# A two-layer encoder trunk: one more fast pair per feed-forward stage, and another order at the stages' edges

## The chip, the cores and the metric

The kernel runs on one core of a Trainium2 chip. The metric is the device time of one execution in microseconds; the figure shown for a kernel is the median of its runs. The profile is of one further execution.

## The reference: what is computed

Two layers work on `x` of 512 tokens by 1024 features, in float32. Each layer is a token mixer (gated linear attention in layer 0, chunked attention in layer 1) and then a feed-forward part, each followed by a LayerNorm of `alpha * x + y`. The change touches the feed-forward part, which both layers have:

```python
def swiglu(x, w_in, w_out):
    gate, up = jnp.split(x @ w_in, 2, axis=-1)
    return (jax.nn.silu(gate) * up) @ w_out
```

`w_in` is 1024 by 5632 (2816 gate columns, 2816 up columns), `w_out` is 2816 by 1024.

## The kernel before

Each float32 operand of a matmul is split into a high part, which ScalarE (ACT) makes by a copy with rounding, and a low part, the difference, made by VectorE (DVE) or GpSimd (POOL). A product is then three matmuls on TensorE (PE): high by high, high by low, low by high (`three`, L1603 to L1605).

**The weight stream.** All weights come in slabs of 128 by 1024, two to a transfer, issued by SyncE into a ring of two places, `raw`. SyncE issues the next transfer when both slabs of the one two before it have their high and low parts (`hi_done`, `lo_done`). The high and low parts lie in rings of four slabs, `w_hi` and `w_lo`. `split_hi` (L497, ACT) and `split_lo` (L967, POOL) are the usual makers. The first four slabs of some stages have places of their own ("early" slabs) and are split ahead of the stage.

**The first half of a feed-forward stage** has 22 pairs of column blocks, one gate and one up block of 128 columns each; a pair is one transfer. The first `PLAIN` = 4 pairs are done the classical way: 2 blocks by 8 depth tiles by 3 matmuls of 512 tokens, 48 matmuls. Pairs 0 and 1 are the early slabs, done in two token halves; pairs 2 and 3 go through the ring. The other `FAST` = 18 pairs are done by a Strassen scheme (Winograd's form): seven products of half the depth and half the tokens, 7 by 4 by 3 = 84 matmuls of 256 tokens. I call them plain and fast pairs.

**What a fast pair needs.** From `x`: four sums of its blocks, formed once a stage on DVE in `sum_x` (L1162 to L1178); the fourth, `t4_sum`, takes L1177 and L1178. ACT makes the high parts of the first three (L579), DVE the low parts (L1301); the fourth gets its high part at L677 (ACT) and its low part at L1313 (DVE), after the last plain pair, because it replaces a block of x that plain pairs still read. From the weights: DVE forms sums (L1201, L1203, L1209, L1212), ACT the high parts (L585 for the gate slab, L589, L593, L597, L601), DVE the low parts (L1218, L1224, L1230, L1235), POOL one low part, `form_a22_low` (L986). These lie in two sets of places, `w_s32` and `w_s4`, by the parity j of the pair.

**The order of products in a fast pair** (PE, `pair`): 1 to bank a, 2 to bank f, 3 to bank a again, 4 to bank e, 5 to bank a, 6 to bank g, 7 to bank a. Bank a is used four times, so ACT copies it out in between: `copy_p1` (L609) after product 1, awaited by product 3; `copy_u2` (L613) after 3, awaited by 5; `copy_u4` (L621) after 5, awaited by 7. The result of 7 is read by `gate_late` (L633). DVE adds the other banks: `gate_of_early` (L1242) feeds ACT's `gate_early` (L625). The engines run ahead by one pair: in `pair(i, j)` ACT and DVE also form the weights of the next pair, in an order that is written out by hand, the same for all pairs but the last.

**The second half** is `out_projection` on 22 slabs of `w_out`. ACT's `hidden_high` (L565) and DVE's `hidden_low` (L1185) split the hidden activations; the high parts lie in a ring of six. The last fast pair of a stage has no next pair: there ACT splits the first slabs of `w_out` and the first hidden blocks. The last four slabs of the second half (`TAIL`) are gone through token tile by token tile. In layer 0 the four early slabs of the next stage are split in its iteration `k = 14`, ahead of those last four.

Of the kernel before, what the change touches and what calls it, by code (L numbers as in the profile page):

```python
# [29 lines left out]
P = 128  # L30
# [52 lines left out]
PLAIN = 4  # L83
# [24 lines left out]
def build_program(nc, a):  # L108
    ctx = ExitStack()
    with ctx:  # L110
# [89 lines left out]
        def halves_at(name, shape, hi, lo):  # L200
# [6 lines left out]
        w_s32 = [halves_at("w_s32_0", [P, 2, HALF], region + 76 * KB, region + 44 * KB),  # L207
                 halves_at("w_s32_1", [P, 2, HALF], region + 68 * KB, gb_at)]
        w_s4 = [halves_at("w_s4_0", [P, HALF], region + 80 * KB, region + 82 * KB),
                halves_at("w_s4_1", [P, HALF], region + 72 * KB, region + 74 * KB)]  # L210
# [198 lines left out]
        def blocks_of(n0, j):  # L409

            slot = (n0 + 2 * j) % RING
            return slot, slot + 1, (n0 // 2 + j) % RAWS
# [59 lines left out]
        def _(act):  # L472
# [55 lines left out]
            def out_projection(n0, slabs, ln):  # L528

                banks = LN_BANKS[ln]  # L530
                for k in range(slabs - TAIL):
                    if slabs == KF and k + HI_RING < KF:
                        hidden_high(ln // 2, k + HI_RING)
# [3 lines left out]
                    split_hi(n0 + k + RING)  # L537

# [28 lines left out]
            def feed_forward(f, n0):  # L567
# [35 lines left out]
                def copy_p1(i, j, start):  # L603
                    act.wait_ge(multiplied[f], i * 12 + (6 * j + 1))
                    if start:
                        act.wait_ge(prod_done[f], PLAIN - 1 + j)
                    else:
                        act.wait_ge(half_prod[f], i * 4 + (2 * j - 3))
# [26 lines left out]
                def pair(i, j, start, before_start, last=False):  # L635
# [11 lines left out]
                    else:  # L647
                        form_s32_high(i_next, j_next)
                        form_s1_high(i_next, j_next)
                        form_a22_high(i_next, j_next)  # L650
                    copy_u2(i, j)
                    if last:
                        split_hi(FFN_OUT[f] + 1)
                        hidden_high(f, 2)
                        hidden_high(f, 3)
                    else:
                        form_s4_high(i_next, j_next)
# [8 lines left out]
                split_hi(n0 + RING + 2)  # L666
                split_hi(n0 + RING + 3)
                gate(2)
# [5 lines left out]
                gate(3)  # L674
# [7 lines left out]
                with act.Fori(2, FAST // 2 - 1) as i:  # L682
                    pair(i, 0, False, False)
                    pair(i, 1, False, False)
                pair(FAST // 2 - 1, 0, False, False)
                pair(FAST // 2 - 1, 1, False, False, True)
                hidden_high(f, 4)
                hidden_high(f, 5)
                gate_late(FAST // 2 - 1, 1, False)
# [260 lines left out]
        def _(pool):  # L950
# [30 lines left out]
            def feed_forward(f, n0):  # L981
# [11 lines left out]
                with pool.Fori(1, FAST // 2) as i:  # L993
                    form_a22_low(i, 0)
                    form_a22_low(i, 1)
                for n in range(n0 + 2 * KF, n0 + 2 * KF + RING):
                    split_lo(n)
# [1155 lines left out]
```

## Time and profile before

| what | us |
|---|---|
| median of 3 runs | 1184.44 (1184.26 to 1184.64) |
| the profiled execution's own time | 1181.81 |
| its span, first to last instruction | 1180.1 |
| PE busy | 1156.9 |
| DVE, ACT, POOL busy | 647.6, 528.2, 419.5 |

The profiled execution's own time is 1.7 us over its span and 2.6 us under the median. The mean granted TensorE clock is 0.997 of full speed. Differences of stretches are read from the trace and taken from the own time; the same difference is then taken from the median.

### The profile page before, as it was taken

The page shows a single profiled execution, that of the slowest core. Times are in us where ns is not written, and L with a number is a line of the kernel's source. Part 1 is how long each engine was busy: PE and PEld are TensorE (multiplying, and loading weights), DVE is VectorE, ACT ScalarE, POOL GpSimd, SP SyncE. Part 2 cuts the span into 40 slices and gives each one's busy share as a digit, 9 for nine tenths or more (in the row PEclk, how much of TensorE's full clock was granted, in tenths as well). Part 3 has the DMA queues.
Part 4 walks back from the last instruction along what each step waited for, and adds up shares of the span by engine and source line. Part 5 has one row for each costly group of instructions (what it writes and reads, how often), then busy time and mean ns, then how long its engine had stood idle before and what let it go on. Part 6 is the DMA issues. An engine that isn't in the chain of part 4 may idle for free.

```text
span 1180.1 us, 18906 instructions
## 1 busy us (share of the span) xinstructions
PE 1156.9 (98%) x6958; PEld 1020.3 (86%) x6958; DVE 647.6 (55%) x1173; ACT 528.2 (45%) x918; POOL 419.5 (36%) x247
## 2 busy tenths in 40 slices
PE   8999999999999999999999999999999999999997
PEld 6887888989999997887887777778989999988886
DVE  4070173788888863112604676636888888841105
ACT  4354253345555553223425666662455555542222
POOL 2438426141111124446245334471311111144441
PEclk9999999999999999999999999999999999999999
DMA  6433314232222233324032212131222333232221
GB/s 217 171 132 107 107 36 143 79 136 101 97 96 101 104 107 143 107 78 172 19 107 72 90 50 85 57 143 60 72 73 107 107 107 107 107 141 80 101 72 72
DMA packets 21977, 119.89 MB, mean 102 GB/s; under 512 B 2449, under 2 KB 6673, under 8 KB 8993
## 3 DMA queue, kind: packets, MB, share of 16 engines
q1 hardware_dynamic: 15440, 104.96, 25.3%
q10 hardware_dynamic: 6480, 14.17, 3.6%
q8 instruction: 37, 0.61, 0.2%
q14 instruction: 20, 0.16, 0.0%
HBM read 117.02 MB, written 5.24 MB: 104 GB/s over the span
## 4 chain that ended last, share of the span: by engine, by line
PE 89%; DVE 4%; ACT 3%; POOL 2%; DMA 1%; issue 1%; SPq 0%; DVEq 0%; POOLq 0%; ACTq 0%
PE bank L1603 27%; PE bank L1605 27%; PE bank L1604 27%; PE bank L1994 2%; PE bank L1979 2%; POOL s_w_lo L967 1%; PE bank L1665 1%; DMA s_raw<-stream 1%; DVE s_g_c L1382 1%; PE bank L2015 1%; PE bank L2014 1%; PE bank L1863 1%; DVE s_a_lo L1185 1%; ACT s_w_hi L497 1%; PE bank L1856 0%
## 5 line engine op out<-in xcount | busy, mean ns | idle before, releaser
L967 POOL TENSOR_TENSOR s_w_lo<-s_raw,s_w_hi 128x1024 fp32r<-128x1024 f32 x108 | 266.1, 2474 | 314.3 <-ACT s_w_hi L497 314.3
L1603 PE MATMUL bank<-s_t_hi,s_w_hi 128*128 128x256 f32 (+1 forms) x832 | 265.7, 319 | 2.8 <-ACT s_gate_s L613 2.2
L1605 PE MATMUL bank<-s_t_hi,s_w_lo 128*128 128x256 f32 (+1 forms) x832 | 263.2, 316 | 0.0
L1604 PE MATMUL bank<-s_t_lo,s_w_hi 128*128 128x256 f32 (+1 forms) x832 | 262.9, 316 | 0.0
L986 POOL TENSOR_TENSOR s_w_lo<-s_raw,s_w_hi 128x512 fp32r<-128x512 f32 x36 | 64.8, 1800 | 307.0 <-ACT s_w_hi L597 307.0
L1603 PEld LDWEIGHTS bank<-s_t_hi,s_w_hi 128*128 128x128 f32 x832 | 158.8, 191 | 12.7 <-DVE s_w_lo L1218 2.5
L1605 PEld LDWEIGHTS bank<-s_t_hi,s_w_lo 128*128 128x128 f32 x832 | 158.7, 191 | 10.5
L1604 PEld LDWEIGHTS bank<-s_t_lo,s_w_hi 128*128 128x128 f32 x832 | 158.9, 191 | 9.3
L497 ACT ACTIVATE s_w_hi<-s_raw 128x1024 fp32r<-128x1024 f32 x111 | 115.6, 1054 | 114.5 <-PE bank L1605 87.1
L1603 PE MATMUL bank<-s_w_hi,s_a_hi 128*128 128x512 f32 x352 | 138.0, 392 | 1.5 <-POOL s_w_lo L967 1.3
L1604 PE MATMUL bank<-s_w_lo,s_a_hi 128*128 128x512 f32 x352 | 137.4, 390 | 0.0
L1605 PE MATMUL bank<-s_w_hi,s_a_lo 128*128 128x512 f32 x352 | 137.3, 390 | 0.0
L1185 DVE TENSOR_TENSOR s_a_lo<-s_act_a,s_a_hi 128x512 fp32r<-128x512 f32 x44 | 36.1, 832 | 168.6 <-ACT s_a_hi L565 168.6
L1603 PE MATMUL bank<-s_t_hi,s_w_s_hi 128*128 128x256 f32 x432 | 122.8, 284 | 4.4 <-ACT s_prod L621 4.4
L1605 PE MATMUL bank<-s_t_hi,s_w_s_lo 128*128 128x256 f32 x432 | 122.7, 284 | 0.0
L1604 PE MATMUL bank<-s_t_lo,s_w_s_hi 128*128 128x256 f32 x432 | 122.7, 284 | 0.0
L1603 PE MATMUL bank<-s_w_hi,s_t_hi 128*128 128x512 f32 x288 | 113.9, 396 | 2.7 <-DVE s_t_lo L1339 1.3
L1605 PE MATMUL bank<-s_w_hi,s_t_lo 128*128 128x512 f32 x288 | 112.3, 390 | 0.0
L1604 PE MATMUL bank<-s_w_lo,s_t_hi 128*128 128x512 f32 x288 | 112.2, 389 | 0.0
L1603 PEld LDWEIGHTS bank<-s_t_hi,s_w_s_hi 128*128 128x128 f32 x432 | 83.3, 193 | 4.8 <-ACT s_prod L621 4.8
L1605 PEld LDWEIGHTS bank<-s_t_hi,s_w_s_lo 128*128 128x128 f32 x432 | 83.3, 193 | 0.0
L1604 PEld LDWEIGHTS bank<-s_t_lo,s_w_s_hi 128*128 128x128 f32 x432 | 83.3, 193 | 0.0
(200 smaller groups left out, 2053.6 us busy)
## 6 DMA issues: line engine op xcount, KB each, us to landing
s_raw<-stream SPq DMA_DIRECT2D x97, 1024.0 KB, 4.7
s_ln_gb<-ln_gb ACTq DMA_DIRECT2D x4, 1024.0 KB, 4.5
bias_rows<-rel_bias ACTq DMA_DIRECT2D x1, 3072.0 KB, 12.4
s_h<-x ACTq DMA_DIRECT2D x1, 2048.0 KB, 12.7
s_r_b<-bias_rows ACTq DMA_DIRECT2D x16, 128.0 KB, 2.3
s_x_t<-x_t ACTq DMA_DIRECT2D x3, 512.0 KB, 11.9
out<-s_h SPq DMA_DIRECT2D x3, 512.0 KB, 2.6
s_raw<-stream SPq DMA_DIRECT2D x2, 256.0 KB, 5.4
```

The lines of the kernel that those rows point to most:

```text
L497: nc.scalar.activation(w_parts(n, slice(0, SLAB))[0], raw[:, pair % RAWS, n % 2, :], ACT.Copy).then_inc(hi_done, 2 if n == 1 else 1)
L967: nc.gpsimd.tensor_tensor(lo, raw[:, place // 2 % RAWS, n % 2, :], hi.bitcast(F32), ALU.subtract).then_inc(lo_done, 2 if n == 1 else 1)
L986: nc.gpsimd.tensor_tensor(w_lo[:, up_at, HALF:], raw[:, slot, 1, HALF:], w_hi[:, up_at, HALF:].bitcast(F32), ALU.subtract).then_inc(lo_don ...
L1185: nc.vector.tensor_tensor(a_lo[:, k, :], act_a[:, k, :], a_hi[k % HI_RING][:, :].bitcast(F32), ALU.subtract).then_inc(a_lo_done[f], 1)
L1382: nc.vector.tensor_tensor_scan(g_c[:, hd, :], keep[:, :], g_c[:, hd, :], 0.0, ALU.mult, ALU.add).then_inc(cum_done, 1)
L1603: nc.tensor.matmul(out, l_hi, r_hi, start=start, stop=False, skip_group_check=skip)
L1604: nc.tensor.matmul(out, l_hi, r_lo, start=False, stop=False, skip_group_check=skip)
L1605: return nc.tensor.matmul(out, l_lo, r_hi, start=False, stop=stop, skip_group_check=skip)
L1665: last = nc.tensor.transpose(bank[banks[t][half]][:, k * P:(k + 1) * P], src[:, t, (4 * half + k) * P:(4 * half + k + 1) * P], ident[:, :])
L1863: last = nc.tensor.matmul(bank[GLA_O_BANKS[t][hd // 2]][:, (hd % 2) * GLA_DV:(hd % 2 + 1) * GLA_DV], g_am[:, t % 2, hd * P:(hd + 1) * P], ...
L1979: last = nc.tensor.matmul(bank[2 + hd][:, keys], qk[q][rows, toks], qk[k][rows, keys], start=(i == 0), stop=(i == 2))
L1994: last = nc.tensor.transpose(bank[4 + hd][:, at * P:(at + 1) * P], r_p[:, s % 4, j * P:(j + 1) * P], ident[:, :])
```

## The change

`PLAIN` goes from 4 to 3, so that each feed-forward stage has 3 plain and 19 fast pairs; the odd last fast pair is written out, and the two sets of places `w_s32` and `w_s4` change roles. The second half of the fourth sum of x becomes `add_x4`, which DVE does after the weights of the first fast pair. In the first fast pair ACT does `copy_u2` ahead of the next pair's high parts. In the last fast pair ACT does `copy_u4` ahead of `gate_early` and of two of the hidden blocks' high parts, and DVE does two `hidden_low` ahead of `gate_of_early` where it did four. In the second half ACT does `split_hi` ahead of `hidden_high` in each iteration; for `k = 14` of layer 0 this puts the four early slabs and the slab itself ahead of `hidden_high`.

```diff
-PLAIN = 4
+PLAIN = 3
...
         def blocks_of(n0, j):
-            slot = (n0 + 2 * j) % RING
-            return slot, slot + 1, (n0 // 2 + j) % RAWS
+            slot = (n0 + 2 * (PLAIN + j)) % RING
+            return slot, slot + 1, (n0 // 2 + PLAIN + j) % RAWS
...
                 for k in range(slabs - TAIL):
-                    if slabs == KF and k + HI_RING < KF:
-                        hidden_high(ln // 2, k + HI_RING)
                     if ln == 1 and k == slabs - 2 * TAIL:
                         for j in range(TAIL):
                             split_hi(n0 + slabs + j)
                     split_hi(n0 + k + RING)
+                    if slabs == KF and k + HI_RING < KF:
+                        hidden_high(ln // 2, k + HI_RING)
...
                 def copy_p1(i, j, start):
                     if start:
-                        act.wait_ge(prod_done[f], PLAIN - 1 + j)
+                        act.wait_ge(prod_done[f], PLAIN)
...
                 def pair(i, j, start, before_start, last=False):
...
                         hidden_high(f, 0)
                         hidden_high(f, 1)
                         split_hi(FFN_OUT[f])
-                    else:
-                        form_s32_high(i_next, j_next)
-                        form_s1_high(i_next, j_next)
-                        form_a22_high(i_next, j_next)
-                    copy_u2(i, j)
-                    if last:
+                        copy_u2(i, j)
                         split_hi(FFN_OUT[f] + 1)
-                        hidden_high(f, 2)
-                        hidden_high(f, 3)
-                    else:
-                        form_s4_high(i_next, j_next)
+                        copy_u4(i, j, start)
+                        gate_early(i, j)
+                        return
+                    if before_start is None:
+                        copy_u2(i, j)
+                    form_s32_high(i_next, j_next)
+                    form_s1_high(i_next, j_next)
+                    form_a22_high(i_next, j_next)
+                    if before_start is not None:
+                        copy_u2(i, j)
+                    form_s4_high(i_next, j_next)
                     gate_early(i, j)
                     copy_u4(i, j, start)
...
                 gate(1)
-                split_hi(n0 + RING + 2)
-                split_hi(n0 + RING + 3)
-                gate(2)
                 form_plain_high(0, 0)
                 form_s32_high(0, 0)
                 form_s1_high(0, 0)
                 form_a22_high(0, 0)
                 form_s4_high(0, 0)
-                gate(3)
+                gate(2)
...
-                pair(FAST // 2 - 1, 0, False, False)
-                pair(FAST // 2 - 1, 1, False, False, True)
-                hidden_high(f, 4)
-                hidden_high(f, 5)
-                gate_late(FAST // 2 - 1, 1, False)
+                pair(FAST // 2, 0, False, False, True)
+                hidden_high(f, 2)
+                gate_late(FAST // 2, 0, False)
+                for k in range(3, HI_RING):
+                    hidden_high(f, k)
                 split_hi(FFN_OUT[f] + 2)
                 split_hi(FFN_OUT[f] + 3)
...
                 own(nc.vector.tensor_tensor(t4_sum[:, :, :], t_hi[:, KD // 2:, EARLY_TOKS].bitcast(F32), t2[:, :, :], ALU.subtract))
+
+            def add_x4(f):
+
                 nc.vector.tensor_tensor(t4_sum[:, :, :], t4_sum[:, :, :], t_lo[:, KD // 2:, EARLY_TOKS].bitcast(F32),
                                         ALU.add).then_inc(x_summed[f], 1)
-                dve.wait_ge(x_summed[f], 4)
...
                     if last:
-                        for k in range(HI_RING - 2):
+                        for k in range(2):
                             hidden_low(f, k)
...
                 plain_prod(1)
-                plain_prod(2)
                 sums_31(0, 0)
                 sums_24(0, 0)
                 form_plain_low(0, 0)
                 form_s32_low(0, 0)
                 form_s1_low(0, 0)
                 form_s4_low(0, 0)
-                plain_prod(3)
+                add_x4(f)
+                plain_prod(2)
                 dve.wait_ge(x_sum_hi[f], 4)
...
-                for c in range(RING):
+                for c in range(2 * PLAIN - RING):
                     pe.wait_ge(lo_done, n0 + RING + c + 1)
```

## Rows read from the trace of the kernel before

**Rows 1.** The page's first part: busy time of each engine, its share, instructions

```profile
PE 1156.9 (98%) x6958; PEld 1020.3 (86%) x6958; DVE 647.6 (55%) x1173; ACT 528.2 (45%) x918; POOL 419.5 (36%) x247
```

**Rows 2.** Waits of PE in the whole run: us in total, times, longest

```profile
PE bank L1603 <- ACT s_prod L621: 4.4, 2, 2.2
PE bank L1603 <- ACT s_gate_s L613: 2.2, 2, 1.1
...
PE bank L1603 <- POOL s_w_lo L967: 2.0, 3, 0.7
```

**Rows 3.** Windows: us, PE, PEld, DVE, ACT, POOL busy (instructions), clock, DMA share, GB/s

```profile
252.35:263.23 10.88, 10.88 (x49) 9.01 (x48) 7.86 (x9) 4.29 (x6) 1.88 (x1) 1.00 0.24 85
263.23:274.61 11.38, 10.30 (x86) 10.12 (x85) 10.26 (x15) 5.96 (x10) 1.89 (x1) 1.00 0.17 50
274.61:284.69 10.08, 10.08 (x87) 10.08 (x86) 8.33 (x14) 5.41 (x10) 1.78 (x1) 1.00 0.36 127
435.89:448.41 12.52, 10.33 (x87) 10.13 (x86) 7.32 (x11) 6.85 (x13) 5.25 (x2) 1.00 0.22 75
546.35:554.14 7.79, 6.32 (x25) 4.28 (x24) 0.00 (x0) 1.99 (x2) 6.26 (x3) 1.00 0.46 144
...
1038.43:1051.63 13.20, 11.01 (x86) 10.80 (x85) 8.01 (x12) 6.85 (x13) 5.25 (x2) 0.94 0.26 95
...
1050.13:1053.40 3.27, 3.27 (x14) 2.88 (x13) 2.07 (x5) 1.80 (x4) 0.13 (x1) 0.50 0.68 286
```

**Rows 4.** Timeline of DVE, start of the fast pairs in layer 0: start, us, line

```profile
240.97 3.31 DVE L1178 TENSOR_TENSOR s_t_sum<-s_t_sum,s_t_lo 128x1024 f32<-128x1024 f32 x1
...
244.92 4.97 DVE L1301 TENSOR_TENSOR s_t_lo<-s_t_sum,s_t_hi 128x1024 fp32r<-128x1024 f32 x3
...
253.16 0.69 DVE L1201 TENSOR_TENSOR s_w_s_sum<-s_raw 128x512 f32<-128x512 f32 x1
...
258.09 1.79 DVE L1230 TENSOR_TENSOR s_w_lo<-s_s_sum,s_w_hi 128x512 fp32r<-128x512 f32 x1
259.80 0.68 DVE L1235 TENSOR_TENSOR s_w_s_lo<-s_w_s_sum,s_w_s_hi 128x512 fp32r<-128x512 f32 x1
...
264.53 1.23 DVE L1313 TENSOR_TENSOR s_t_lo<-s_t_sum,s_t_hi 128x1024 fp32r<-128x1024 f32 x1 [0.40 <-ACT s_t_hi L677]
...
270.60 0.41 DVE L1242 TENSOR_TENSOR s_gate_s<-s_gate_s,bank 128x256 f32<-128x256 f32 x1
```

**Rows 5.** Timeline of ACT, the same stretch

```profile
255.21 1.06 ACT L589 ACTIVATE s_w_s_hi<-s_w_s_sum 128x1024 fp32r<-128x1024 f32 x1 [1.24 <-DVE s_w_s_sum L1209]
...
263.43 1.06 ACT L677 ACTIVATE s_t_hi<-s_t_sum 128x1024 fp32r<-128x1024 f32 x1 [4.84 <-PE bank L1605]
...
265.35 0.36 ACT L609 ACTIVATE s_gate_s<-bank 128x256 f32<-128x256 f32 x1
...
269.72 0.36 ACT L613 ACTIVATE s_gate_s<-bank 128x256 f32<-128x256 f32 x1
```

**Rows 6.** Timeline of POOL, the same stretch

```profile
240.39 6.15 POOL L967 TENSOR_TENSOR s_w_lo<-s_raw,s_w_hi 128x1024 fp32r<-128x1024 f32 x2 [0.54 <-ACT s_w_hi L497]
257.44 1.88 POOL L986 TENSOR_TENSOR s_w_lo<-s_raw,s_w_hi 128x512 fp32r<-128x512 f32 x1 [10.90 <-ACT s_w_hi L597]
```

**Rows 7.** Timelines of DVE and ACT, last fast pair of layer 0

```profile
442.29 3.48 DVE L1185 TENSOR_TENSOR s_a_lo<-s_act_a,s_a_hi 128x512 fp32r<-128x512 f32 x2 [2.53 <-ACT s_a_hi L565]
...
446.46 0.36 ACT L621 ACTIVATE s_prod<-bank 128x256 f32<-128x256 f32 x1
```

**Rows 8.** Timelines of ACT and POOL, end of layer 0's second half

```profile
530.77 1.99 ACT L497 ACTIVATE s_early<-s_raw 128x1024 fp32r<-128x1024 f32 x2
...
541.60 1.06 ACT L497 ACTIVATE s_w_hi<-s_raw 128x1024 fp32r<-128x1024 f32 x1 [5.83 <-DMA s_raw<-stream]
...
542.74 9.87 POOL L967 TENSOR_TENSOR s_w_lo<-s_raw,s_w_hi 128x1024 fp32r<-128x1024 f32 x4 [1.37 <-ACT s_w_hi L497]
```

**Rows 9.** The page's DMA issues: count, KB each, us to landing

```profile
s_raw<-stream SPq DMA_DIRECT2D x97, 1024.0 KB, 4.7
```

More of the change, by code:

```diff
@@ L206, in build_program @@
                   for name, hi, lo in (("t1", 48, 52), ("t2", 56, 60), ("t3", 64, 84))}
[L207 to L210, printed above, removed]
+        w_s32 = [halves_at("w_s32_0", [P, 2, HALF], region + 68 * KB, gb_at),
+                 halves_at("w_s32_1", [P, 2, HALF], region + 76 * KB, region + 44 * KB)]
+        w_s4 = [halves_at("w_s4_0", [P, HALF], region + 72 * KB, region + 74 * KB),
+                halves_at("w_s4_1", [P, HALF], region + 80 * KB, region + 82 * KB)]
         t4_sum = sb_at("t4_sum", [P, KD // 2, SEQ // 2], F32, prod_at)
@@ L681, in feed_forward @@
                 pair(1, 1, False, False)
-                with act.Fori(2, FAST // 2 - 1) as i:
+                with act.Fori(2, FAST // 2) as i:
                     pair(i, 0, False, False)
                     pair(i, 1, False, False)
-                pair(FAST // 2 - 1, 0, False, False)
-                pair(FAST // 2 - 1, 1, False, False, True)
-                hidden_high(f, 4)
-                hidden_high(f, 5)
-                gate_late(FAST // 2 - 1, 1, False)
+                pair(FAST // 2, 0, False, False, True)
[3 more added lines that the diff above has]
+                    hidden_high(f, k)
                 split_hi(FFN_OUT[f] + 2)
@@ L995, in feed_forward @@
                     form_a22_low(i, 1)
+                form_a22_low(FAST // 2, 0)
                 for n in range(n0 + 2 * KF, n0 + 2 * KF + RING):
@@ L1316, in feed_forward @@
                 pair(0, 1, True)
-                with dve.Fori(1, FAST // 2 - 1) as i:
+                with dve.Fori(1, FAST // 2) as i:
                     pair(i, 0, True)
                     pair(i, 1, True)
-                pair(FAST // 2 - 1, 0, True)
-                pair(FAST // 2 - 1, 1, True, True)
-                up_of_late(FAST // 2 - 1, 1)
-                up_of_early(FAST // 2 - 1, 1)
-                hidden_early(FAST // 2 - 1, 1)
-                for k in range(HI_RING - 2, HI_RING):
-                    hidden_low(f, k)
-                hidden_late(FAST // 2 - 1, 1)
-                for k in range(HI_RING, KF):
+                pair(FAST // 2, 0, True, True)
+                up_of_late(FAST // 2, 0)
+                up_of_early(FAST // 2, 0)
+                hidden_early(FAST // 2, 0)
+                hidden_low(f, 2)
+                hidden_late(FAST // 2, 0)
+                for k in range(3, KF):
                     hidden_low(f, k)
@@ L1798, in feed_forward @@
                     pair(i, 1, False)
+                pair(FAST // 2, 0, False)
             pe.wait_ge(am_zeroed, 1)
```

## The prediction

> **What bounds the kernel now.** I read the page's busy times first: PE is busy 98% of the span, the next engine 55% [rows 1]. So time is had only by giving PE less work, or by filling its idle stretches. Second come the waits of PE, for the whole run: three kinds belong to places that the change touches, the longest two of them twice each, once per layer [rows 2]. PE waits for `copy_u4` (L621), 2.2 us a time, for `copy_u2` (L613), 1.1 us a time, and for `split_lo` (L967), some of it at the end of layer 0's second half. Third, the windows put a price on each place, as start-to-start time of PE's work, which also holds what an idle stretch costs beside the idle itself [rows 3]. A fast pair in the middle takes 10.08 us; the first one of layer 0 takes 11.38, the last one 12.52, the last one of layer 1 13.20. Last, the timelines of DVE, ACT and POOL at these places say who was late and behind what [rows 4 to 8].
>
> **1. One plain pair becomes a fast pair.** Plain: 10.88 us for 48 matmuls of 512 tokens. Fast: 10.08 us for 84 of 256 [rows 3]. That is -0.80 us a layer, -1.6 in all. The fast pair brings 14 DVE instructions (8.33 us) and 10 of ACT (5.41), both under 10.08, so the steady state hides them; the transfers are the same slabs. Swapping the two sets of places costs nothing: it puts the last pair (now j = 0) again on the set that the hidden blocks' ring does not overlap. The Trainium skill's page "TensorE: Matmul & The Clock Gate", section "Back-to-back issue gap", gives N/2.4 + 2.5 ns a matmul when nothing else binds, 109 ns at 256 and 216 at 512. By it the exchange would be worth 1.19 us a layer instead of 0.80, and the total 0.8 us lower; the rows have 120 and 227 ns, and I go by them.
>
> **2. The start of the fast pairs.** Today the first fast pair loses 11.38 - 10.08 = 1.30 us: DVE forms the second pair's sums only after L1313, so ACT's L589 is late, and `copy_u2` stands behind it at 269.72, where product 5 was ready to start at 268.99 (four products of 1.44 us after 263.23) [rows 3, 5]. The change puts `copy_u2` in front, and this loss goes: -1.3 a layer.
>
> But the first fast pair now starts 10.88 us earlier, at 252.35, and its preparation must be there. I lay DVE out again from 240.97, where L1178 started [rows 4]. `plain_prod(0)` takes it to 241.6. The three L1301 took 4.97 us because POOL held them up until 246.54 (240.39 + 6.15) [rows 4, 6]; those two POOL instructions are the splits of plain pair 3 and are gone. Alone such an instruction takes 1.23 (L1313) [rows 4] and the next starts after 1.14, so three end at 245.0. The Trainium skill, "SBUF — State Buffer", section "SBUF: two separate sides", calls the port pair of VectorE and GpSimd an exclusive lock for two-input instructions. If the lock were not what stretched the three, they would still take 4.97 and everything below would be 1.55 us later in each layer; the rows (blocked to POOL's end, then 1.1 each) fit the lock.
>
> `plain_prod(1)` ends at 245.6. The chain that began at 253.16 follows, 7.56 us earlier; all it waits for is there, since the raw slabs were the old pair 3's. POOL's L986 moves with it to 249.9 and holds L1230 as before (1.79). L1235 moves from 259.80 to 252.24 and ends near 252.85. Only then comes `add_x4`, 1.2 us, done at 254.05. That is late: ACT could start L677 0.2 us after the pair's start (263.43 against 263.23), thus at 252.55, and now starts at 254.1. Queued behind it on ACT are L585 and `copy_p1`, which comes 1.92 us after L677 (265.35 against 263.43): at 256.0, done at 256.4, PE 0.15 later. Product 3 could start at 255.23. So **a new wait of 1.3 us for `copy_p1`** takes the place of the one removed. `plain_prod(2)`, which `copy_p1` now also needs, falls into the gap (254.0 to 254.7).
>
> Behind that, L1313 is at 255.2 (1.10 after L677), and L1242, which came 6.07 us after it, at 261.3. `gate_early` and `copy_u4` follow in 1.1 us, at 262.4; product 7 could start at 262.3. That is 0.2 more with the restart, and DVE enters the second pair about 0.9 us later than in steady state, where it has 10.08 - 8.33 = 1.75 us of slack: 0.2 more, and then it has recovered. With 0.1 for the slower restart, the new loss is 1.8 us against 1.30: **+0.5 a layer, +1.0 in all**. Bounds for the new loss: 0 (the sum is ready in time) and 1.8 + 1.55 = 3.4 a layer. In total from -2.6 to +4.2. I take 1.8, the direct layout.
>
> **3. The end of the fast pairs.** In the last pair DVE's two later `hidden_low` ran from 442.29 for 3.48 us, held up by POOL's splits; `gate_of_early` stood behind them, `gate_early` behind that, `copy_u4` behind that at 446.46 [rows 7]. Product 7 could have started 6 x 1.44 = 8.64 us after 435.89, at 444.53. In the new order ACT reaches `copy_u4` after the second slab split, which ends 5.8 us into the pair; product 5 ends at 7.2, so the copy is done at about 7.8, before 8.64. Nothing on DVE stands ahead of it. What is moved back, `hidden_high` 2 to 5 and the splits of slabs 2 and 3, is wanted from 2 x 5.44 us into the second half on (24 matmuls of 0.227 a slab), and comes within some 4.5 us of ACT work after its start; POOL adds 2.4 a slab. `gate_late`, wanted by the second token tile 1.36 us in, comes at 0.2 and takes 0.4. So the full 12.52 - 10.08 = **-2.44 in layer 0**. In layer 1 the same wait is followed by a granted clock of 0.50, that is 1.2 GHz, from 1050.13 to 1053.40 [rows 3]: half of 3.27 us is lost, 1.6. PE had been idle 2.2 us before it fell, and without that idle it should not: **-2.44 - 1.6 = -4.0 in layer 1**. Bounds: -4.9 (the clock falls anyway, in one way or another) and -8.1 (the timed runs have the fall in both layers and lose it). I take -6.5.
>
> **4. The end of layer 0's second half.** The stretch from slab 18 to 21 of the first token tile is 24 matmuls, 5.44 us, and took 7.79: 2.35 lost to POOL's four low parts, back to back from 542.74 to 552.6 [rows 3, 8]. They start late because ACT splits the early slabs only after `hidden_high(20)`, which waits for slab 14, and the two-place raw ring passes this delay on: 4.7 us for a transfer [rows 9], and ACT sat idle 5.83 us for it at 541.60. In the new order the first two early slabs, long landed, are split right after the previous iteration, whose ACT work ends at 526.3 (530.77 - 5.44 + 1.0). POOL then has slab 17 until 528.3 and two early slabs at 2.4 until 533.0 (today 536.7: 541.60 less the 4.7 and 0.2 to issue), the next transfer lands at 538.0, the low parts of slabs 18 and 19 end at 543.9, slab 20's at 547.5, slab 21's at 550.1. Slab 21 waits for slab 17's matmuls, so it is not earlier. PE wants them at 549.07 and 550.43. So **-2.2**, bounds -2.35 and -1.0. `hidden_high(20)` slides to about 539 and its low part to 542, wanted at 549.07. In layer 1 no early slabs follow and PE does not wait there.
>
> **Sum.** -1.6 + 1.0 - 6.5 - 2.2 = -9.3 us. The profiled execution's own time goes from 1181.8 to 1172.5, the median from 1184.4 to **1175.1**.
>
> **Rivals.**
> - *No new wait at the start.* If `add_x4` is there when ACT wants it, the 1.8 a layer go: 1175.1 - 3.6 = 1171.5. Against it: DVE's layout has no idle time to win back. Chance 0.13.
> - *One gain fails.* The clock's fall stays, or the second half's end stays as it is, or the start wait is at its upper bound (+3.2): 1177 to 1181, middle 1178.5. For it: each is a bound worked out above. Chance 0.2.
> - *The end wait only moves.* PE then waits as long for a hidden block or a slab of the second half; parts 3 and 4 give nothing: -0.6, 1183.8, no change. Against it: the margins above are microseconds. Chance 0.05.
> - *Slower.* DVE never recovers its lag: it enters each fast pair 0.9 us late, and if the lag stayed above its slack of 1.75, PE would lose the excess in each of 38 fast pairs. It decides from 9.3 / 38 = 0.25 us a pair; at 0.5 the result is 1175.1 + 19 = 1194. For it: DVE is the fullest engine beside PE in a fast pair, and every wait of the start passes through it. Against it: the pair after the first today is already 10.08 us, after a DVE stretch of 10.26 us busy in 11.38 [rows 3]. Chance 0.05.
>
> **How the numbers follow.** My forecast has 0.57, with its own range 1173 to 1177. The range 1171 to 1180.5 holds it, nearly all of the first rival and most of the second, some 0.83. About 0.2% (2.4 us) is what a measurement can tell from no change. Faster by more: 0.57 + 0.13 + 0.18 = 0.88. Within: 0.06. Slower: 0.06.
>
> **What would show it.** In the new trace: PE's wait for L621's successor and for L613's at zero at the ends; a wait of PE for `copy_p1` of 1.1 to 1.3 us, twice; the three L1301 in 3.5 us; last fast pairs of 10.1 us in both layers; no stretch at 1.2 GHz inside the stages; the early slabs' splits some 4 us ahead of slab 14's last matmul, and PE's waits for L967 down from three to one. I am wrong if PE waits for another engine in the first microseconds of a second half, if middle pairs exceed 10.08, or if the first pair takes over 13.5.

## The result, and the profile after

The median goes from 1184.35 us (4 runs of before on the same chip, 1183.48 to 1184.64) to **1172.81 us** (4 runs, 1172.51 to 1174.24): ratio 0.9906, 95% interval 0.9889 to 0.9923. The profiled execution's own time (one of the four) is 1173.0, its span 1171.2. One run of the kernel before in a later series took 1627.58 us at a mean granted clock of 0.654; it is left out of every median, ratio and range here. The prediction was 1175.1, with a range of 1171 to 1180.5. The direction, the size and nearly every step came out; one term, the clock behind the long waits, was taken too small for the median, and one small loss at the start was not there.

The page's first part, to be read beside [rows 1]:

```profile
span 1171.2 us, 19196 instructions
...
PE 1152.8 (98%) x7030; PEld 1021.0 (87%) x7030; DVE 704.3 (60%) x1199; ACT 533.7 (46%) x932; POOL 411.5 (35%) x245
```

PE's busy time falls by 4.1 us only, and the span by 8.9: more than half of what is gained was idle time. PE's waits in the whole run (us in total, times, longest) answer to [rows 2]:

```profile
PE bank L1603 <- ACT s_gate_s L609: 2.1, 2, 1.1
...
PE bank L1603 <- POOL s_w_lo L966: 1.3, 2, 0.7
```

`copy_u4` (L621) and `copy_u2` (L613) are gone from the list. `copy_p1` (L609) has come in, twice, 1.1 us each. Of the two waits left for `split_lo` (now L966), neither lies in a second half; they are at 100.95 and 197.81 us, ahead of layer 0's feed-forward stage.

The windows, in the columns of [rows 3], in this order: last plain pair, first, second and last fast pair of layer 0; the tail of its second half; last fast pair of layer 1 and the stretch behind it.

```profile
242.20:253.09 10.89, 10.89 (x51) 9.00 (x49) 10.82 (x13) 4.17 (x6) 1.87 (x1) 1.00 0.24 94
253.09:264.79 11.70, 10.53 (x85) 10.15 (x84) 11.04 (x16) 5.85 (x10) 1.84 (x1) 1.00 0.29 97
264.79:274.87 10.08, 10.08 (x86) 10.08 (x85) 9.19 (x16) 5.41 (x10) 1.79 (x1) 1.00 0.43 150
436.15:446.23 10.08, 10.08 (x86) 10.08 (x85) 4.02 (x9) 5.29 (x10) 4.77 (x2) 1.00 0.10 32
544.18:549.65 5.47, 5.47 (x26) 4.47 (x24) 0.00 (x0) 1.06 (x1) 3.88 (x2) 1.00 0.55 192
...
1033.61:1043.69 10.08, 10.08 (x86) 10.08 (x85) 4.02 (x9) 5.29 (x10) 4.77 (x2) 1.00 0.10 36
1043.69:1047.00 3.31, 3.31 (x17) 2.74 (x16) 2.64 (x5) 3.11 (x6) 0.13 (x1) 1.00 0.99 347
```

Both last fast pairs take 10.08 us, where they took 12.52 and 13.20; the granted clock behind them is 1.00, where it was 0.50 in layer 1. The tail takes 5.47 for 7.79. The first fast pair takes 11.70 for 11.38, and the second is already undisturbed.

**Where 8.85 us of the span went.** I take the start of each stretch from PE's first matmul in it, in both traces, up to PE's last matmul (1172.01 before, 1163.17 after), and subtract:

| stretch | change, us |
|---|---|
| a plain pair becomes a fast one, 2 x (10.08 - 10.88) | -1.60 |
| loss of the first fast pair, 2 x (1.62 - 1.30) | +0.64 |
| last fast pair, 2 x (10.08 - 12.52) | -4.88 |
| clock from the last fast pair of layer 1 on | -1.59 |
| layer 0, second half's start to layer 1's first fast pair, less one plain pair | -2.16 |
| ahead of layer 0's first fast pair, less one plain pair | +0.74 |
| sum | -8.85 |

The last line is a shift ahead of the stage and not of the change. 0.63 us of it is PE's wait for a low part, up to the matmul at 197.81. Start to start, less one matmul, that wait costs 0.77 us here and 0.14 in the first trace of before, and it differs between executions of one kernel: two further traces of before have 0.60 and 0.83, a second one of after 0.74. The start of the first fast pair moves with it, roughly: less a plain pair, it is at 252.35 in the first trace of before, at 252.76 and 252.98 in the two further ones, and at 253.09 and 252.97 in the two of after.

### The profile page after: what moved, and what is told of

Read it like the earlier page. It is cut to its first block, busy times and chain, and to the rows that moved or that the text cites. A ratio compares the mean times of both kernels' runs of the same rounds, so it can differ in the third digit from the quotient of the medians.

```text
span 1171.2 us, 19196 instructions
## 1 busy us (share of the span) xinstructions
PE 1152.8 (98%) x7030; PEld 1021.0 (87%) x7030; DVE 704.3 (60%) x1199; ACT 533.7 (46%) x932; POOL 411.5 (35%) x245
## 4 chain that ended last, share of the span: by engine, by line
PE 84%; DVE 8%; ACT 3%; POOL 2%; issue 2%; DMA 1%; SPq 0%; DVEq 0%; POOLq 0%; ACTq 0%
PE bank L1603 26%; PE bank L1605 26%; PE bank L1604 26%; PE bank L1995 2%; PE bank L1980 2%; DMA s_raw<-stream 1%; DVE s_g_c L1382 1%; PE bank L2016 1%; PE bank L2015 1%; PE bank L1665 1%; POOL s_early L966 1%; POOL s_w_lo L966 1%; ACT s_g_on L777 1%; DVE s_t_sum L1177 1%; DVE s_bn_o L1454 0%
## 5 line engine op out<-in xcount | busy, mean ns | idle before, releaser
L966 POOL TENSOR_TENSOR s_w_lo<-s_raw,s_w_hi 128x1024 fp32r<-128x1024 f32 x104 | 254.0, 2453 | 313.7 <-ACT s_w_hi L497 313.7
L1603 PE MATMUL bank<-s_t_hi,s_w_hi 128*128 128x256 f32 (+1 forms) x832 | 262.0, 315 | 0.7 <-POOL s_w_lo L966 0.7
L985 POOL TENSOR_TENSOR s_w_lo<-s_raw,s_w_hi 128x512 fp32r<-128x512 f32 x38 | 68.5, 1803 | 315.6 <-ACT s_w_hi L597 315.6
L1187 DVE TENSOR_TENSOR s_a_lo<-s_act_a,s_a_hi 128x512 fp32r<-128x512 f32 x44 | 84.7, 1938 | 108.5 <-ACT s_a_hi L565 108.4
L1603 PE MATMUL bank<-s_t_hi,s_w_s_hi 128*128 128x256 f32 x456 | 129.4, 284 | 2.3 <-ACT s_gate_s L609 2.1
L1604 PE MATMUL bank<-s_t_lo,s_w_s_hi 128*128 128x256 f32 x456 | 129.0, 283 | 0.0
L1605 PE MATMUL bank<-s_t_hi,s_w_s_lo 128*128 128x256 f32 x456 | 129.0, 283 | 0.0
L1603 PEld LDWEIGHTS bank<-s_t_hi,s_w_s_hi 128*128 128x128 f32 x456 | 87.5, 192 | 3.1 <-ACT s_gate_s L609 2.5
L1604 PEld LDWEIGHTS bank<-s_t_lo,s_w_s_hi 128*128 128x128 f32 x456 | 87.5, 192 | 0.0
L1605 PEld LDWEIGHTS bank<-s_t_hi,s_w_s_lo 128*128 128x128 f32 x456 | 87.5, 192 | 0.0
## 6 DMA issues: line engine op xcount, KB each, us to landing
s_raw<-stream SPq DMA_DIRECT2D x2, 256.0 KB, 5.3
```

Of the source, the lines that this page charges most:

```text
L966: nc.gpsimd.tensor_tensor(lo, raw[:, place // 2 % RAWS, n % 2, :], hi.bitcast(F32), ALU.subtract).then_inc(lo_done, 2 if n == 1 else 1)
L985: nc.gpsimd.tensor_tensor(w_lo[:, up_at, HALF:], raw[:, slot, 1, HALF:], w_hi[:, up_at, HALF:].bitcast(F32), ALU.subtract).then_inc(lo_don ...
L1187: nc.vector.tensor_tensor(a_lo[:, k, :], act_a[:, k, :], a_hi[k % HI_RING][:, :].bitcast(F32), ALU.subtract).then_inc(a_lo_done[f], 1)
L1603: nc.tensor.matmul(out, l_hi, r_hi, start=start, stop=False, skip_group_check=skip)
L1604: nc.tensor.matmul(out, l_hi, r_lo, start=False, stop=False, skip_group_check=skip)
L1605: return nc.tensor.matmul(out, l_lo, r_hi, start=False, stop=stop, skip_group_check=skip)
```

## The experiments

Eight edits, in two groups: parts of the change on top of before, and steps away from the changed kernel. The kernel before was run beside each, in three series of 22, 8 and 9 runs with medians of 1183.37, 1184.1 and 1184.06. Its runs gather in two groups: of the 22, nine lie at 1181.9 to 1182.6, ten at 1184.2 to 1184.9 and three between. So ratios are given, against runs of both groups.

### The last fast pair's order alone

On before, ACT's and DVE's order in the last fast pair as in the change, the two `hidden_high` behind it too:

```diff
                         split_hi(FFN_OUT[f])
...
+                        copy_u2(i, j)
+                        split_hi(FFN_OUT[f] + 1)
+                        copy_u4(i, j, start)
+                        gate_early(i, j)
+                        return
...
                     copy_u2(i, j)
-                    if last:
-                        split_hi(FFN_OUT[f] + 1)
-                        hidden_high(f, 2)
-                        hidden_high(f, 3)
...
                     if last:
-                        for k in range(HI_RING - 2):
+                        for k in range(2):
                             hidden_low(f, k)
```

> The kernel before with the order of the last fast pair alone changed (copy_u4 ahead of gate_early and of two hidden blocks; two hidden_low ahead of gate_of_early instead of four); four plain pairs as before. Theory A, the clock falls at the stage's end in layer 1 only: the last fast pairs take 10.1 us instead of 12.5 and 13.2, -2.44 in layer 0 and -4.07 in layer 1, 6.5 us off the median. Theory B, the timed executions of before lose the clock in both layers, which would explain why their median stands 2.5 us over the profiled one: 8.1 us off, or a little more. Theory C, the wait only moves to a hidden block or a slab of the second half: under 1 us off.

Measured 1176.33 us (1175.79 to 1176.79), ratio 0.994 (0.9927 to 0.9954), that is -7.0 us. Windows of the last fast pairs of both layers:

```profile
437.19:447.27 10.08, 10.08 (x86) 10.08 (x85) 4.03 (x9) 5.29 (x10) 4.78 (x2) 1.00 0.11 38
...
1037.42:1047.50 10.08, 10.08 (x86) 10.08 (x85) 4.02 (x9) 5.30 (x10) 4.78 (x2) 1.00 0.10 39
```

This one order is three fifths of the whole gain. It is worth more than the 4.88 us of waits that it takes out of the windows. The rest fits the clock: in this trace the granted clock doesn't fall inside a stage, and in those of before it falls once or twice, at about 1.6 us a fall (below). The spread of the runs shrinks with it as well, from 3 us to 1.

### The changed kernel with the old order at that place

ACT's order, and with it DVE's four `hidden_low` ahead of `gate_of_early`:

```diff
                         split_hi(FFN_OUT[f] + 1)
+                        hidden_high(f, 2)
+                        hidden_high(f, 3)
+                        gate_early(i, j)
                         copy_u4(i, j, start)
-                        gate_early(i, j)
                         return
...
                     if last:
-                        for k in range(2):
+                        for k in range(HI_RING - 2):
                             hidden_low(f, k)
```

> The changed kernel with the last fast pair in the old order. Theory A: the waits of 2.2 us before product 7 come back in both layers, 2.44 us each; the clock may fall behind them in one, both or neither layer, 1.6 us each: 4.9 to 8.1 us slower than the changed kernel. If the fall needs the idle stretch, a stretch at half clock shows behind these waits and nowhere else inside the stages. Rival: the clock falls for another reason, then it is as rare as in the changed kernel and the cost is 4.9.

Measured 1179.24 us (1178.42 to 1181.57), ratio 0.9964 (0.995 to 0.9978): 6.4 us over the changed kernel. PE's wait is back, and the clock's fall with it, this time in layer 0 and not in layer 1 (the windows behind the last pair of each):

```profile
PE bank L1605 <- ACT s_prod L621: 4.6, 2, 2.3
```

```profile
447.30:450.60 3.30, 3.30 (x15) 3.17 (x15) 2.22 (x6) 1.25 (x4) 0.00 (x0) 0.53 0.66 278
1048.50:1051.50 3.00, 3.00 (x19) 2.74 (x20) 2.53 (x6) 2.18 (x5) 0.00 (x0) 1.00 0.82 336
```

The two windows are one code, one cause and one length of wait; in the one the clock fell and in the other it didn't. So the cost of this wait differs from execution to execution.

### Two more profiles of the kernel before

No edit: what do the two levels of before's times, some 1182 and some 1184.4, consist of?

> The kernel before, one look, to see in which stages the clock falls in another execution. Theory B: an execution near 1184 us shows stretches at half clock behind both waits for L621, one near 1182 us behind one of them only. Rival: the same single fall as in the first profile, then the time above 1182 us is lost elsewhere.

> The same as the other look at the kernel before: the number of stretches at half clock goes with the time, about 1.6 us each.

The first took 1182.21 us, the second 1184.12. The windows behind the waits of the last pairs, layer 0 and layer 1, the first execution's, then the second's:

```profile
449.00:452.30 3.30, 3.30 (x16) 2.69 (x16) 1.09 (x3) 2.28 (x3) 1.86 (x1) 1.00 0.92 330
...
1051.50:1054.50 3.00, 3.00 (x9) 2.39 (x9) 1.20 (x3) 2.27 (x3) 1.14 (x1) 0.54 0.75 265
```

```profile
449.00:452.30 3.30, 3.30 (x11) 2.67 (x10) 1.36 (x3) 2.27 (x3) 1.38 (x1) 0.53 0.86 340
...
1053.40:1056.30 2.90, 2.90 (x9) 2.32 (x9) 1.23 (x3) 2.27 (x3) 1.09 (x1) 0.50 0.77 308
```

One fall in the faster execution, two in the slower; 0.47 of 3.3 us is 1.55, and the times differ by 1.9. The profile shown ahead of the prediction (1181.8) was an execution with a single fall, and the runs behind the median are of the group near 1184.4. That all of that group have two falls is the plain reading; their traces weren't taken, and their mean granted clock (0.995 to 0.997, against 0.997 near 1182) orders them only roughly.

### The slab splits ahead of `hidden_high` alone

```diff
-                    if slabs == KF and k + HI_RING < KF:
-                        hidden_high(ln // 2, k + HI_RING)
...
                     split_hi(n0 + k + RING)
+                    if slabs == KF and k + HI_RING < KF:
+                        hidden_high(ln // 2, k + HI_RING)
```

> The kernel before with split_hi ahead of hidden_high in the second half alone. Theory A: the early slabs are split 4 us sooner, the four low parts at the end of layer 0's second half come in time, and the stretch from slab 18 to 21 takes 5.44 us instead of 7.79: 2.35 us off. Rival: the raw ring's transfers set the time of the low parts, not ACT's order, then the waits for L967 stay and nothing changes (within 0.3 us).

Measured 1179.28 us (1178.26 to 1180.49), ratio 0.9969 (0.9957 to 0.998): -3.7 us, interval -2.4 to -5.1, where the expectation was 2.35 and the trace of the changed kernel has 2.16. PE's waits at the tail are gone in this trace (what is left is at 101.63 and 198.05), and nothing else in it is faster:

```profile
PE bank L1603 <- ACT s_prod L621: 4.4, 2, 2.2
...
PE bank L1603 <- POOL s_w_lo L967: 0.9, 2, 0.7
```

The sign and the place are confirmed; some 1.5 us of the measured gain has no place in the trace. Compared trace with trace, one fall in each, the profiled executions are 1180.42 against 1181.81 and 1182.21, and the stretch from the second half's start to layer 1's first fast pair is 415.49 us (450.49 to 865.98) for 417.36, with part of a fall inside it. The remainder is of the size of one clock fall, and the number of falls differs between executions of one kernel; no run shows that the splits' order changes it.

### `copy_u2` first in the first fast pair alone

```diff
+                    if before_start is None:
+                        copy_u2(i, j)
...
                     form_s32_high(i_next, j_next)
                     form_s1_high(i_next, j_next)
                     form_a22_high(i_next, j_next)
-                    copy_u2(i, j)
+                    if before_start is not None:
+                        copy_u2(i, j)
```

> The kernel before with copy_u2 ahead of the next pair's high parts in the first fast pair alone. Theory A: the wait of PE before product 5 goes and the first fast pair takes 10.1 to 10.2 us instead of 11.38 in both layers, 2.5 us off in all. Rival: the wait moves to product 7, because gate_early, ahead of copy_u4 on ACT, hangs on the same late DVE chain: then a wait of 0.3 to 1 us for L621 shows in the first fast pair, and 1 to 2 us come off.

Measured 1180.35 us (1178.46 to 1181.16), ratio 0.9973 (0.9964 to 0.9983), -3.2 us. The window of the first fast pair of layer 0:

```profile
264.71:274.80 10.09, 10.09 (x85) 10.07 (x84) 9.41 (x14) 5.86 (x10) 1.58 (x1) 1.00 0.11 28
```

The window stops 0.05 us short: by the first matmuls of the pair and of the next one (264.71, 274.85) 11.38 has become 10.14, and PE waits at this place for neither L613 nor L621. So, with four plain pairs, the copy's place is 1.24 of the 1.30 us, 2.5 in both layers. The measured 3.2 is 0.7 more, for which the trace, with one clock fall as in the first of before, shows no place.

### Three plain pairs with all the old orders

`PLAIN = 3`, the odd pair written out and the sets of places swapped, as in the change; the fourth sum, the two last-pair orders, `copy_u2` and the slab splits as before:

```diff
-PLAIN = 4
+PLAIN = 3
```

> Three plain and nineteen fast pairs, but every order as in the kernel before: x's fourth sum whole in sum_x, copy_u2 behind the next pair's high parts, the old last pair, hidden_high first in the second half. Theory A: the exchange itself gives 2 x 0.80 us; the first fast pair then starts while DVE is 2 to 3 us behind it, copy_u2 ends 8 to 9 us into the pair where product 5 wants it at 5.8, so the first pair loses 2.5 to 3 us instead of 1.3. In all 0.8 to 1.8 us slower than before. Rival: with less contention from GpSimd DVE is there in time, the first pair loses 1.3 as before, and the kernel is 1.6 us faster.

Measured 1183.54 us (1182.2 to 1187.25), ratio 1.0002 (0.9992 to 1.0012): nothing. PE's waits, a window behind the wait at the start of the fast pairs, and the first matmul behind that wait:

```profile
PE bank L1599 <- ACT s_prod L621: 4.6, 2, 2.3
...
PE bank L1599 <- ACT s_gate_s L613: 3.9, 2, 1.9
```

```profile
261.50:265.00 3.50, 3.50 (x19) 3.50 (x19) 2.44 (x5) 0.80 (x2) 0.87 (x1) 0.53 0.38 105
```

```profile
260.78 0.36 PE L1599 MATMUL bank<-s_t_hi,s_w_hi 128*128 128x256 f32 x1 [1.94 <-ACT s_gate_s L613]
```

The exchange still saves its 1.6 us (the pairs in the middle take 10.08), and the start takes them back. The wait is now 2.10 us, counted from when its matmul was due (258.68 to 260.78), and was 1.24 before (268.99 to 270.23). The whole first fast pair takes 12.39 us in layer 1 (858.85 to 871.24), where the clock stayed at 1.00, so it loses 2.31 us instead of 1.30, 2.0 more in both layers. That is under the 2.5 to 3 of the expectation, and the kernel is no slower. The profiled execution is 2.2 us over the median; the clock fell in it behind the wait shown and behind both waits of the last pairs. The number of fast pairs is worth something only together with the orders at the edge.

### The fourth sum of x early

On the changed kernel, `t4_sum` again whole in `sum_x`, ahead of the plain pairs' products:

```diff
-            def add_x4(f):
-
                 nc.vector.tensor_tensor(t4_sum[:, :, :], t4_sum[:, :, :], t_lo[:, KD // 2:, EARLY_TOKS].bitcast(F32),
...
+                dve.wait_ge(x_summed[f], 4)
...
-                add_x4(f)
                 plain_prod(2)
```

> The changed kernel with x's fourth sum finished in sum_x again, ahead of the first pair's weights. Theory A: ACT starts its high part 0.2 us into the first fast pair instead of 1.8, copy_p1 is in time (plain_prod(2) ends 2.3 us in, product 3 wants the copy at 2.9), the wait of 1.1 us before product 3 goes. DVE reaches gate_of_early about 8.4 us in, so copy_u4 ends at about 9.5 and product 7 waits 0.8 to 1 us: 0.5 to 0.9 us a layer off, 1.0 to 1.8 faster than the changed kernel. Rival: the first pair's weights come too late for product 1 or 2, because DVE is 1.14 us later with them: then a wait for a low part of weights shows at the pair's start, and the kernel is not faster.

Measured 1172.38 us (1171.31 to 1173.04), ratio 0.9905 (0.9889 to 0.9921), within 0.5 us of the changed kernel. Timelines of ACT and PE in the first fast pair of layer 0:

```profile
252.76 1.06 ACT L676 ACTIVATE s_t_hi<-s_t_sum 128x1024 fp32r<-128x1024 f32 x1 [0.56 <-PE bank L1602]
...
261.38 0.42 ACT L625 ACTIVATE s_gate_s<-s_gate_s 128x256 f32<-128x256 f32 x1 [0.70 <-DVE s_gate_s L1242]
261.71 0.37 ACT L621 ACTIVATE s_prod<-bank 128x256 f32<-128x256 f32 x1
```

```profile
262.22 0.36 PE L1600 MATMUL bank<-s_t_hi,s_w_s_hi 128*128 128x256 f32 x1 [0.72 <-ACT s_prod L621]
```

The wait for `copy_p1` is gone, and product 7 waits 0.72 us instead (0.88 from start to start), for `copy_u4`, which stands behind `gate_early`. The first fast pair takes 11.17 us (first matmul to the next pair's first) where it took 11.71. So of some 1.6 us a layer 0.54 is saved in the trace, and of the 1.09 left 0.88 is this wait: DVE has the same work before `gate_of_early`, whichever end the sum stands at. That is 1.1 us in both layers, in the expected range of 1.0 to 1.8; the medians differ by 0.4 us only, and the two ranges of runs overlap.

### `copy_u4` first too, then both copies in two pairs

On top of the last one, `copy_u4` ahead of `gate_early` in the first fast pair:

```diff
+                    if before_start is None:
+                        copy_u4(i, j, start)
                     gate_early(i, j)
-                    copy_u4(i, j, start)
+                    if before_start is not None:
+                        copy_u4(i, j, start)
```

> The same as the run with the fourth sum early, and copy_u4 ahead of gate_early in the first fast pair. Theory A: copy_u4 then waits for product 5 alone and ends 7.8 us in, product 7 does not wait: the first fast pairs take 10.1 us, 1.6 us a layer less than in the changed kernel, 3.3 us in all. Rival: DVE's lag shows in the second fast pair, which then waits 0.3 to 1 us for copy_u2 or gate_early: 2 to 3 us in all.

Measured 1171.8 us (1170.79 to 1172.02), ratio 0.9896 (0.988 to 0.9912). That is about 1 us less than the changed kernel, where the expectation had 3.3 and its rival 2 to 3. Product 7's wait is gone and the first fast pair takes 10.23 us, but the second pair takes 10.79, with a wait that shows in PE's timeline and in ACT's:

```profile
270.04 0.36 PE L1603 MATMUL bank<-s_t_hi,s_w_hi 128*128 128x256 f32 x1 [0.49 <-ACT s_gate_s L613]
```

```profile
267.52 1.06 ACT L589 ACTIVATE s_w_s_hi<-s_w_s_sum 128x1024 fp32r<-128x1024 f32 x1 [1.88 <-DVE s_w_s_sum L1212]
...
269.53 0.36 ACT L613 ACTIVATE s_gate_s<-bank 128x256 f32<-128x256 f32 x1
```

It is the kernel before's own wait once more, one pair later: DVE is late with L1212, ACT's L589 waits for it, and `copy_u2` stands in the queue behind. The rest was then to put both copies first in the second pair as well:

```diff
-                    if before_start is None:
+                    if start:
                         copy_u2(i, j)
...
-                    if before_start is not None:
+                    if not start:
                         copy_u2(i, j)
                     form_s4_high(i_next, j_next)
-                    if before_start is None:
+                    if start:
                         copy_u4(i, j, start)
                     gate_early(i, j)
-                    if before_start is not None:
+                    if not start:
                         copy_u4(i, j, start)
```

> The run with the fourth sum early and copy_u4 first, and both copies (copy_u2 and copy_u4) first in the second fast pair too. Theory A: the wait of 0.5 us before product 5 of the second pair (0.66 start to start, 0.1 for the restart) goes in both layers, since copy_u2 no longer stands behind high parts that wait for DVE: no wait of PE above 0.2 us is left in the fast pairs, 1.5 us less than that run, 2.5 to 3.3 less than the changed kernel. Rival: DVE's lag of about 1 us is only handed on, and the third pair waits for copy_u2 or copy_u4 by 0.3 to 0.7 us.

Measured **1169.94 us** (1169.44 to 1171.27), ratio 0.9886 (0.9869 to 0.9903). The changed kernel, run again beside it:

> The changed kernel once more, as the base for the run beside it, and for its scatter. Theory A: without the idle stretches of 2.2 us the clock never falls inside a stage, so its executions lie within 1.7 us of each other, where those of before scatter over 3 us.

It took 1172.86 us (1172.44 to 1173.0), ratio 0.9909 (0.9895 to 0.9922): five runs within 0.6 us of each other, and no clock fall inside a stage. The last version is 2.9 us under it, and the fastest of all. All 19 fast pairs of layer 0 in one window, and ACT in the second one:

```profile
253.38:445.05 191.67, 191.67 (x1598) 191.56 (x1596) 158.53 (x264) 104.18 (x190) 37.34 (x21) 1.00 0.29 104
```

```profile
268.13 0.38 ACT L613 ACTIVATE s_gate_s<-bank 128x256 f32<-128x256 f32 x1 [2.50 <-PE bank L1605]
268.41 1.05 ACT L589 ACTIVATE s_w_s_hi<-s_w_s_sum 128x1024 fp32r<-128x1024 f32 x1
```

19 x 10.08 is 191.52; 0.15 us is left. `copy_u2` now waits for PE (2.50 us idle, released by the bank), and no longer PE for it. DVE is as late as before: its lag has only stopped reaching PE.

## Why the prediction was right, and where it was off

**1. The exchange, -1.6.** Right: 10.89 and 10.08 in the windows after, [rows 3] before. The gap that the Trainium skill gives for an isolated matmul ("TensorE: Matmul & The Clock Gate", section "Back-to-back issue gap"), N/2.4 + 2.5 ns, would have made it 1.19 us a layer. These pairs don't follow it: 10.88 us for 48 matmuls and 10.08 for 84 are 227 and 120 ns each, and give 0.80.

**2. The start, +1.0.** The mechanism and the places were right to a fraction of a microsecond. DVE, ACT and PE after, layer 0:

```profile
242.31 3.49 DVE L1303 TENSOR_TENSOR s_t_lo<-s_t_sum,s_t_hi 128x1024 fp32r<-128x1024 f32 x3
...
253.55 1.21 DVE L1181 TENSOR_TENSOR s_t_sum<-s_t_sum,s_t_lo 128x1024 f32<-128x1024 f32 x1
...
255.95 1.23 DVE L1315 TENSOR_TENSOR s_t_lo<-s_t_sum,s_t_hi 128x1024 fp32r<-128x1024 f32 x1 [0.59 <-ACT s_t_hi L676]
...
262.02 0.41 DVE L1244 TENSOR_TENSOR s_gate_s<-s_gate_s,bank 128x256 f32<-128x256 f32 x1
```

```profile
254.85 1.06 ACT L676 ACTIVATE s_t_hi<-s_t_sum 128x1024 fp32r<-128x1024 f32 x1 [3.39 <-DVE s_t_sum L1181]
...
256.76 0.36 ACT L609 ACTIVATE s_gate_s<-bank 128x256 f32<-128x256 f32 x1
```

```profile
257.18 0.38 PE L1603 MATMUL bank<-s_t_hi,s_w_s_hi 128*128 128x256 f32 x1 [1.06 <-ACT s_gate_s L609]
```

Everything here lies 0.74 us later than in the prediction's frame, by the waits ahead of the stage. Less that, `add_x4` ends at 254.02 (predicted 254.05), L676 starts at 254.11 (254.1), `copy_p1` at 256.02 (256.0), `gate_of_early` at 261.28 (261.3). The three low parts take 3.49 us (3.5) where they took 4.97 [rows 4]: POOL's splits are gone from this stretch, and nothing else holds DVE up. The Trainium skill ("SBUF — State Buffer", section "SBUF: two separate sides") calls the port pair that VectorE and GpSimd share an exclusive lock for two-input instructions, and the trace agrees with it: 3.49 us with POOL idle, 4.97 beside its splits. **The loss is 1.62 us a layer, not 1.8**: 1.3 at product 3 with its restart, and 0.3 at product 7 with its own, as predicted together (1.3, 0.1, 0.2); the term that was off is the 0.2 us for the second pair, which takes 10.08. So +0.64 in place of +1.0. Against the old orders at three plain pairs (2.31 a layer), the new ones are worth 0.69 a layer. The last experiments show what holds the rest: mostly not `add_x4`, whose place is worth 0.54 a layer and decides which product waits, but copies of PE's banks that stand behind ACT instructions which wait for a late DVE.

**3. The end, -6.5.** Right in its mechanism. In the last pair of layer 0 ACT waits for PE now, and DVE stands ahead of nothing that PE wants:

```profile
443.56 0.38 ACT L621 ACTIVATE s_prod<-bank 128x256 f32<-128x256 f32 x1 [1.55 <-PE bank L1605]
443.83 0.41 ACT L625 ACTIVATE s_gate_s<-s_gate_s 128x256 f32<-128x256 f32 x1
```

The copy starts 7.41 us into the pair (436.15), and product 7 wants it at 8.64. The windows give -2.44 in layer 0. In layer 1 they give -3.12, since the fall began inside the 13.20 us; the traces of the slab splits alone and of `copy_u2` alone, with no fall there, have 12.52 and 12.53 us for this pair. No wait took its place in the second half. **The clock's part was mis-sized for the median.** The prediction had the two bounds, -4.9 and -8.1, and chose -6.5, which is what the two traces show (-4.88 - 1.59). But the profile of before had one fall, and of the four runs behind before's median three (1184.26 to 1184.64) are of the slower group, some 2 us above, and the fourth (1183.48) lies between the groups. The extra profile with two falls is of the slower group too. For these runs the far bound, -8.1, is the nearer one. Against 22 runs of both groups this order alone gave -7.0.

**4. The tail, -2.2.** Measured -2.16. ACT and POOL at the end of the second half, after:

```profile
524.17 1.99 ACT L497 ACTIVATE s_early<-s_raw 128x1024 fp32r<-128x1024 f32 x2
...
536.25 1.06 ACT L497 ACTIVATE s_w_hi<-s_raw 128x1024 fp32r<-128x1024 f32 x1 [3.03 <-DMA s_raw<-stream]
...
544.44 1.06 ACT L497 ACTIVATE s_w_hi<-s_raw 128x1024 fp32r<-128x1024 f32 x1 [1.20 <-PE bank L1605]
```

```profile
526.19 5.20 POOL L966 TENSOR_TENSOR s_early<-s_raw,s_early 128x1024 fp32r<-128x1024 f32 x2
...
543.32 4.74 POOL L966 TENSOR_TENSOR s_w_lo<-s_raw,s_w_hi 128x1024 fp32r<-128x1024 f32 x2 [0.72 <-ACT s_w_hi L497]
```

The second half starts 2.18 us earlier than before (446.23 for 448.41). With that added, the early slabs' splits start at 526.35 (predicted 526.3), POOL ends the second early one at 533.6 (533.0; two take 5.20 us and not 4.8), the next slab is there at 538.4 (538.0), slab 21's low part ends at 550.2 (550.1). ACT's wait for the transfer is 3.03 us where it was 5.83 [rows 8]. The prediction had PE's waits for the low parts of slabs down from three to one; two are left, and the second, at 197.81, is the one whose length differs between executions.

**The sum.** By the traces -1.60 + 0.64 - 4.88 - 1.59 - 2.16 = -9.6, against -9.3 predicted; the profiled execution shows -8.8, since it met 0.74 us more ahead of the stage. For the median, 1175.1 predicted and 1172.8 measured, 2.3 us apart: 0.36 is the start, and about 1.6 fits the second clock fall that the profile of before didn't have. That the runs behind the median had it is not shown, as their traces weren't taken. What is left, some 0.3 us, is less than the interval (4 us wide) can tell.

**The rivals.** The end wait did not move, no gain failed, and DVE caught up within one pair. The rival with no wait at the start was wrong as stated, and its point holds in a way: 2.9 us more are to be had there, by an order and not by DVE having time.

## What to carry to other kernels

On an engine whose instructions run in order, an instruction that frees a PE bank goes ahead of one that waits for a third engine; look for this at a pipeline's edges, where the steady state's hand-written order meets late inputs, and follow the lag into the second iteration too, since a mended wait comes back there. An idle stretch of PE can cost more than its length, so price it from start to start and in more than one execution. And an exchange that saves busy time (here 1.6 us) can be worth nothing until the edge it moves is looked at: alone it gave a ratio of 1.0002.

## What the runs showed of the hardware

**The same wait is followed by a clock fall in one execution and by none in the next.** Over all profiles, the last pair's waits of 2.2 to 2.3 us came with a fall of the granted clock to about 0.5 (1.2 GHz) for some 3 us in 9 of 14 cases, in either layer; the waits of 1.9 us at the start of the fast pairs in one of 2; those of 1.1 us in none of 16. In the six profiles with none of the two longer kinds (the changed kernel twice, the last-pair order alone, and the three versions with the fourth sum early) the clock was at 1.00 from 12 us to PE's last matmul. A fall costs about 1.6 us: from the last fast pair's start in layer 1 on, less the wait's 2.44, the three traces of before, each with a fall there, take 1.58 to 1.60 us more than that of the last-pair order alone. The edited kernels that have the long waits spread over 2.2 to 5 us, and those without them over 0.6 to 1.8. The kernel before spread over 3.1 us in 22 runs and 3.7 in nine, though 1.7 in eight and 1.2 in four.

**VectorE and GpSimd.** Three subtractions of 128 by 1024 took 3.49 us with POOL free and 4.97 beside its splits [rows 4]; the additions that read a PE bank took 0.41 us with POOL busy too (L1242 at 270.60 [rows 4], L1244 at 262.02; POOL's `form_a22_low` ran from 269.95 for 1.89 us and from 261.41 for 1.84), and 0.41 with POOL idle (L1252 at 272.91).
